# A weight ring in which the low part takes the raw chunk's place

## The reference

```python
# layer 0: attention in a window of 128 with a sink per head, 32 heads, 4 key/value heads
mix = swa_sink_attention(h, w_in, b_in, sinks, w_o, b_o)
# layer 1: compressed, selected and windowed attention, weighted by sigmoid gates
mix = gate0 * o_cmp + gate1 * o_sel + gate2 * o_win ; mix @ w_o
# both layers: causal convolution of width 3 over the gate branch, d_ff 5632
a = causal_dwconv(h @ w_gate, conv_w, conv_b)
y = (silu(a) * (h @ w_up)) @ w_down
```

## Time and profile before

| | |
|---|---|
| median of 3 runs | 2115.01 us (2114.51 to 2116.24) |
| profiled execution, span from first to last instruction | 2113.3 us |
| TensorE busy / VectorE / ScalarE / GpSimd | 100% / 63% / 50% / 14% |
| granted TensorE clock | 1.000 of full speed |
| DMA, mean over the span | 180 GB/s, 54% of 16 engines' time on the SP queue |

### The profile page before, as it was taken

One profiled execution on the slowest core, in us unless ns is written; L12 is line 12 of the kernel. 1 busy time (PEld: TensorE's weight loads), 2 busy tenths in 40 slices (PEclk: granted clock), 3 DMA queues, 4 the chain that ended last, 5 costly groups with the idle time before them and its releaser, 6 DMA issues.

```text
span 2113.3 us, 34635 instructions
## 1 busy us (share of the span) xinstructions
PE 2104.6 (100%) x12177; PEld 1803.3 (85%) x12177; DVE 1336.3 (63%) x2048; ACT 1064.2 (50%) x1627; POOL 286.4 (14%) x461
## 2 busy tenths in 40 slices
PE   9999999999999999999999999999999999999999
PEld 9987888888888888888999977888888888888887
DVE  7665676766766754445876654576766767754444
ACT  6675554444444444434666776554444444444443
POOL 4452000000000000000065773000000000000000
PEclk9999999999999999999999999999999999999999
DMA  7444455555565565554773334455565565565554
GB/s 256 151 159 154 166 194 194 181 191 187 172 204 181 187 213 187 188 188 155 235 251 121 101 111 135 155 200 189 179 193 184 180 199 186 182 215 190 188 187 133
DMA packets 111008, 381.42 MB, mean 180 GB/s; under 512 B 14194, under 2 KB 18754, under 8 KB 110402
## 3 DMA queue, kind: packets, MB, share of 16 engines
q1 hardware_dynamic: 108466, 373.63, 53.6%
q10 hardware_dynamic: 2448, 6.53, 0.9%
HBM read 377.97 MB, written 2.14 MB: 180 GB/s over the span
## 4 chain that ended last, share of the span: by engine, by line
PE 97%; DVE 1%; ACT 1%; DMA 0%; issue 0%; ACTq 0%; DVEq 0%
PE set L764 32%; PE set L842 30%; PE set L768 16%; PE set L1058 10%; PE set L1132 2%; PE set L900 1%; PE set L1106 1%; PE set L1154 1%; PE set L932 1%; PE set L1108 1%; PE set L1156 0%; PE set L974 0%; DVE wlo L1851 0%; PE set L1222 0%; PE set L1223 0%; DMA raw<-in_stream 0%
## 5 line engine op out<-in xcount | busy, mean ns | idle before, releaser
L1851 DVE TENSOR_TENSOR wlo<-raw,whi 128x1024 fp32r<-128x1024 f32 x703 | 859.9, 1233 | 560.1 <-ACT whi L1389 558.3
L1389 ACT ACTIVATE whi<-raw 128x1024 fp32r<-128x1024 f32 x703 | 736.9, 1056 | 725.8 <-PE set L768 351.2
L764 PE MATMUL set<-hs,whi 128*128 128x512 f32 x2896 | 952.7, 395 | 0.6 <-ACT whi L1487 0.3
L768 PE MATMUL set<-hs,wlo 128*128 128x256 f32 x2896 | 681.9, 281 | 0.0
L768 PEld LDWEIGHTS set<-hs,wlo 128*128 128x128 f32 x2896 | 534.8, 188 | 60.0 <-DVE wlo L1851 0.2
L764 PEld LDWEIGHTS set<-hs,whi 128*128 128x128 f32 x2896 | 497.2, 189 | 69.8 <-issue 0.8
L842 PE MATMUL set<-whi,hid 128*128 128x512 f32 x1360 | 374.6, 395 | 0.0
L842 PEld LDWEIGHTS set<-whi,hid 128*128 128x128 f32 x1360 | 255.1, 188 | 63.6 <-DVE wlo L1851 0.6
L842 PE MATMUL set<-wlo,hid 128*128 128x512 f32 x680 | 215.8, 395 | 0.0
L1058 PE MATMUL set<-hs,whi 128*128 128x256 f32 x1280 | 213.3, 286 | 0.3 <-DVE wlo L1851 0.3
L1058 PEld LDWEIGHTS set<-hs,whi 128*128 128x128 f32 x1280 | 176.6, 189 | 3.0 <-DVE wlo L1851 1.1
(11 more groups left out here) (219 smaller groups left out, 1449.0 us busy)
## 6 DMA issues: line engine op xcount, KB each, us to landing
raw<-in_stream SPq DMA_DIRECT2D x703, 512.0 KB, 3.4
gain_rows<-rows ACTq DMA_DIRECT2D x4, 1024.0 KB, 5.9
xT<-in_x SPq DMA_DIRECT2D x8, 256.0 KB, 7.7
out_y<-out_f SPq DMA_DIRECT2D x8, 256.0 KB, 2.4
bo_rows<-rows ACTq DMA_DIRECT2D x1, 768.0 KB, 9.1
wg_raw<-in_w_gates ACTq DMA_DIRECT2D x1, 768.0 KB, 4.6
raw<-in_stream SPq DMA_DIRECT2D x2, 256.0 KB, 4.3
bo_last<-rows ACTq DMA_DIRECT2D x1, 256.0 KB, 11.7
```

The source lines that it names most:

```text
L764: return mm(sets[set_of(u)][:, t, 0:2 * w], whi[:, slot, cols], r, start=first, stop=final)
L768: return mm(sets[set_of(u)][:, t, w:2 * w], wlo[:, slot, cols], r[:, 0:w], start=False, stop=False)
L1389: A(whi[:, slot, :], raw[:, slot, :], ACT.Copy).then_inc(hi_ready, 1)
L1851: V.tensor_tensor(wlo[:, slot, :], raw[:, slot, :], whi[:, slot, :].bitcast(F32), ALU.subtract).then_inc(lo_ready, 1)
```

## The change

`wlo` is put at the address of `raw`, slot by slot: `raw` is opened in a scope that closes at once, and `wlo`, of the same size, is the next tile. VectorE's subtraction then writes the low part over the raw chunk that it reads, number by number at the same place. Since the slot now holds the low part until TensorE is done with it, each fetch waits for `chunk_used` of the chunk four before instead of `lo_ready`. ScalarE's, VectorE's and TensorE's instructions and waits stay as they are. SBUF has 16 KB more free in each partition, which nothing takes.

```diff
-        raw = sb("raw", [RING, CW])
+        with ExitStack() as c:
+            raw = sb("raw", [RING, CW], F32, c)
+        wlo = sb("wlo", [RING, CW], F32R)
         whi = sb("whi", [RING, CW], F32R)
-        wlo = sb("wlo", [RING, CW], F32R)
...
             for s in range(RING):
-                sp.wait_ge(lo_ready, s + 1)
+                sp.wait_ge(chunk_used, s + 1)
                 sp.dma_start(raw[:, s, :], stream[RING + s]).then_inc(raw_in[s], 16)
...
-                        sp.wait_ge(lo_ready, n * RING + (lo - RING + s + 1))
+                        sp.wait_ge(chunk_used, n * RING + (lo - RING + s + 1))
                         sp.dma_start(raw[:, s, :], turns[n + lo // RING, s]).then_inc(raw_in[s], 16)
...
-                    sp.wait_ge(lo_ready, g - RING + 1)
+                    sp.wait_ge(chunk_used, g - RING + 1)
                     sp.dma_start(raw[:, g % RING, :], stream[first_chunk(o + k) + c]).then_inc(raw_in[g % RING], 16)
...
-                sp.wait_ge(lo_ready, g - RING + 1)
+                sp.wait_ge(chunk_used, g - RING + 1)
                 sp.dma_start(raw[:, g % RING, :], stream[first_chunk(u) + c]).then_inc(raw_in[g % RING], 16)
```

## The result

The changed kernel took 2265.97 us (median of 5, 2258.87 to 2270.68) against 2114.59 for the kernel before: 1.0708 times as long, 95% interval 1.0697 to 1.0720. A second series gave 2259.58 (2257.88 to 2262.45), ratio 1.0691 (1.0676 to 1.0705). So the direction held, and so did the mechanism at most places, while the sum was much too small: 92 us of the 145 to 151 measured.

The account below looks back on a forecast made before the run. The prediction took TensorE to bound the kernel, busy 2104.6 of 2113.3 us. Its terms, 24+9+30+9+2+10+8 = 92 us, on the unchanged kernel's 2115.0 gave 2207 us, range 2155 to 2265.

Parts of the forecast that it names:

- the ring chain: Per slot: issue, landing, high part, low part take 5.9 us, against 8.4 us of cover from three other FFN chunks.
- the pair's end: At 22 FFN pair ends the low part of chunk 4 comes 1.1 us late behind waiting splits: 24 us.
- layer 1's blocks: Eleven attention blocks in layer 1's query units: a turn waits 2.7 us for ScalarE's copy behind a split, 30 us.
- the mixed stage: Where VectorE builds compressed blocks: late fetches beside weight loads and short compression chunks cost 10 us, bounds 5 and 18.
- layer 1's output pair: Five attention blocks in layer 1's output unit at 1.8 us each, 9 us, plus 3 us for broadcast loads.
- the norms: Three norm transitions: the first parts of h start 2.9 us later behind a split waiting for its fetch, 9 us.
- the broadcast load: Row loads at each output pair's start slow a fetch that ScalarE now waits for: 5 us layer 0, 3 layer 1.
- rival two: TensorE's clock falls to 1.2 GHz after each of some forty idle gaps, doubling a chunk's time: 2322 us, chance 0.06.
- layer 0's attention: Layer 0's turns are a whole chunk apart, so 2 us, bounds 0 and 10; broadcast loads there add 5 us.
- One: Rival: the four-slot ring hides every fetch, so the kernel is not slower: 2115 us, chance 0.06.
- Three: Rival: fetches settle at landings of 4.6 us everywhere, the mixed stage's median: 2263 us, chance 0.09.
- Four: Rival: landings of 3.0 us and ScalarE catching up in half of the blocks: 2156 us, chance 0.09.

Follow-up runs that it names:

- the two experiments on it: Changed kernel with raw and low-part buffers apart again, 2262.08 us; in-place write with eight slots for raw and low part, four for high parts, 2114.35 us.
- half a fetch: Low parts in their own memory, refill waiting for the last product, each fetch bringing only the first half of a chunk: 2202.93 us, ratio 1.0429.
- two new orders: Changed kernel with evacuation and addition ahead of a split at FFN pair ends, 2229.45 us; every second layer 1 split after the fourth copy, 2220.56; both, 2195.32.
- Eight and four slots: Changed kernel's in-place write with eight slots for raw and low part and four for high parts: 2114.35 us, ratio 0.9999 to the kernel before.
- the wait alone: Changed kernel with low parts in their own 16 KB again, the refill still waiting for the chunk's last product: 2262.08 us, ratio 1.0689.

## Why the direction was right, and where the size failed

*Right: the in-place write costs nothing* (1230 ns, and the two experiments on it), *the ring chain* of landing, high part and low part, *and the pair's end.* With U = 658.7 in the changed kernel the prediction's chain can be laid over the trace of ScalarE and VectorE:

```profile
659.44 1.06 ACT L1390 ACTIVATE whi<-raw 128x1024 fp32r<-128x1024 f32 x1 [1.66 <-DMA raw<-in_stream]
660.41 1.01 ACT L1402 ACTIVATE half<-set 128x1024 f32<-128x1024 f32 x1
662.16 1.06 ACT L1390 ACTIVATE whi<-raw 128x1024 fp32r<-128x1024 f32 x1 [0.74 <-DMA raw<-in_stream]
667.01 1.06 ACT L1821 ACTIVATE hid<-gate 128x1024 f32 x1 [3.79 <-DVE gate L2462]
```
```profile
661.68 1.41 DVE L1879 TENSOR_TENSOR gate_in<-half,set 128x256 f32<-128x256 f32 x4
663.26 1.23 DVE L1852 TENSOR_TENSOR wlo<-raw,whi 128x1024 fp32r<-128x1024 f32 x1 [0.17 <-ACT whi L1390]
...
668.43 1.23 DVE L2464 TENSOR_TENSOR hid<-gate,hid 128x1024 f32 x1 [1.55 <-ACT hid L1821]
669.57 3.49 DVE L1852 TENSOR_TENSOR wlo<-raw,whi 128x1024 fp32r<-128x1024 f32 x3
```

U is here the end of the up unit. The split of chunk 2 was forecast at U+0.8 and stands at U+0.7, the addition at U+3.0 (3.0), the low part of chunk 3 at U+4.75 (4.6), that of chunk 4 done at U+12.3 (12.1). TensorE wanted it at U+11.2 and waited 0.96. The 22 pair ends cost 19.4 + 4.1 = 23.5 us of waits, forecast 24. The wait of the eleventh stands at the first chunk of the down projection (2.1 and 2.0 us); the rest of the down projections has next to none, as forecast.

*Right: layer 1's blocks.* Forecast 11 waits of 2.7; in the query units the eleven over 0.5 us come to 26.3, most of them 2.0 to 2.6. One of them, TensorE and ScalarE:

```profile
1224.78 0.28 PE L1059 MATMUL set<-hs,wlo 128*128 128x256 f32 x1
1227.54 0.69 PE L1133 MATMUL set<-ident,probs 128*128 128x128 f32 x2 [2.48 <-ACT turned L1583]
```
```profile
1226.05 1.06 ACT L1390 ACTIVATE whi<-raw 128x1024 fp32r<-128x1024 f32 x1 [2.78 <-DMA raw<-in_stream]
1227.01 0.47 ACT L1583 ACTIVATE turned<-set 128x384 f32<-128x384 f32 x1
```

The copy stands behind the split, the split behind the fetch, as the prediction read it out of the earlier trace rows. *Right in the sum, by luck in part:* the mixed stage (10 forecast, 10.1 of waits), layer 1's output pair (12 and 12.1) and the norms (9 and 9.8). In the mixed stage the fetch beside the weight loads did come late (6.2 us), but TensorE waited 2.6 behind the blocks, where 6 were forecast, and eleven times 0.2 to 1.6 further on, where 4 were. In the output pair no fetch took more than 4.3 us and the 3 us for the broadcast load were not there; the blocks cost more instead. At the norms the forecast mechanism gave 5.9, and two waits of 2.0 for rnorm were not in the working.

*Wrong, the largest part: a wait was priced at its length.* The sum held 92 us of waits and nothing else. Measured are 112 of waits and 34 on top of them. Of these, about 20 are the clock: the prediction said that it "stays at 1.000", and of its rival two that nothing spoke for it. It fell eleven times in the first profile, each time beside a wait of 1.4 us or more, of which there were some 35; the shorter waits at the pair ends brought none there. Rival two had the kind right and the size wrong: not after each wait and not for a chunk's length, but 20 us instead of its 115. The trace of before could not show it, since its longest wait is 1.1 us. A term between nothing and rival two's 115 us belonged in the sum. The page that the prediction named beside this rival, the Trainium skill's "TensorE: Matmul & The Clock Gate", section "HAM oscillation — how this bites in real kernels", tells of waits between groups of matmuls that throttle the engine again and again. The traces agree in kind (eleven falls in this profile), not in each wait. The other 14 us are what a wait takes beyond the idle time shown. At a pair's end of the changed kernel:

```profile
391.85 0.39 PE L765 MATMUL set<-hs,whi 128*128 128x512 f32 x1
392.08 0.40 PE L769 MATMUL set<-hs,wlo 128*128 128x256 f32 x2
393.85 0.73 PE L765 MATMUL set<-hs,whi 128*128 128x512 f32 x2 [1.38 <-DVE wlo L1852]
```

The two products from 392.08 on would have been followed by the next one 0.24 later, as the row is spaced elsewhere; it starts at 393.85, 1.5 late, while the row counts 1.38 of idle time from the modelled end of the last product, and the first two after the wait take 0.73 where two take 0.63 elsewhere. Over the ten pairs of layer 0 the stretch is 13.1 us longer with 10.6 of waits and no fall of the clock: 0.25 for each wait. With half a fetch the same stretch is 7.9 longer with 5.3 of waits, so that it is again 0.26 for each, though the waits are half as long.

*Wrong: layer 0's attention, where 2 us and 5 for the broadcast loads were forecast and 18 of waits came.* The step that failed is "in layer 0 the turns are a whole chunk apart": I looked at turns alone. The queries' bias stands behind a split as well, four times, 8.3 us in all. Beside the row loads two fetches landed in 5.9 and 5.2 us, and one turn behind the first waited 3.3, where 5 were forecast. Another turn of the output pair waited 2.3 behind a split whose fetch took its usual 3.3, and 3.4 of waits are for tiles that GpSimd masks.

*Wrong: the last two output units, where nothing was forecast and 6.6 of waits came.* In each layer, at their start, the y of the units before is late behind splits (2.5 and 2.3 us).

*The rivals.* One fell: TensorE's idle time isn't 9 us but 121. Three reached nearly the measured time, 2263, for a reason that isn't there: the landings stayed at 3.3 in the long runs. Four fell, as neither the landings nor the blocks were as quick as it took.

## What to carry to other kernels

A longer-held buffer is priced by what is queued behind the instruction that waits for its refill, on that engine and the next, against the room each of these has; the engine's own waiting time says little (777 us of it cost 5 us, 1002 cost 150). Look through every place where another operation stands behind that instruction, not the repeating one alone, and add to each wait of TensorE about 0.2 us, as here, and a share for the clock where waits are as long as those beside which it fell here. Before paying with time for memory, look at the order behind the wait: two new orders brought back 64 to 71 of the 145 to 151 us with the 16 KB still free. Eight and four slots lost nothing, but they take the memory of the kernel before.

## What the runs showed of the hardware

- The granted clock fell to 1.2 GHz beside some waits of TensorE of 1.4 us and more and not beside others of the same length: the same program had a mean clock of 0.991 and 0.989 in two profiles, and its runs spread by 0.5%, where the kernel before spreads by 0.1%. In layer 1's query units the loss followed the length of the waits: with waits of about 2.4 us at ten or eleven turns they showed 0.90 to 0.95, with 1.7 they showed 0.98 and with none at the turns 1.00. The two stretches not shown above are those of the wait alone and of half a fetch:

```profile
1180.40:1346.30 165.90, 135.08 (x1063) 0.90 0.24 77
```
```profile
1157.40:1302.40 145.00, 124.74 (x1063) 0.98 0.15 45
```

- A fetch of 256 KB landed in 2.6 us, one of 512 KB in 3.3.
- Fetches that TensorE paced did not land later than fetches issued as early as could be: in the long runs the median was 3.3 us instead of 3.4, and in the output pairs the slowest took 5.9 us instead of 9.1.
